# Entry of a mixture of experts: ranks by pairs, turns in three operations, squares in pieces, tokens scaled from copies

## The reference, cut to what matters

```python
x = x + g1 * mixed                                   # mixed: attention out @ w_out
hx2 = modulate(rmsnorm(x, norm_ffn_g[l]), sh2, sc2)
x = x + g2 * hierarchical_moe(hx2, ...)
# in hierarchical_moe, t = tokens x 1024
g_logits = t @ w_rg + b_rg;  g_sel = argmax(g_logits)
e_logits = (t @ w_re + b_re)[group g_sel]
top_p, top_i = top_k(softmax(e_logits), 2);  top_p /= sum(top_p)
hid = silu(t @ wg) * (t @ wu);  y = sum over experts of (hid * combine) @ wd
```

## Time and profile before

| | us |
|---|---|
| time, median of 3 runs | 772.77 |
| lowest, highest | 772.65, 773.9 |
| profiled execution, its own time | 772.82 |
| its span, first to last instruction | 770.9 |

### The profile page before, as it was taken

How to read it: one execution, slowest core, us unless ns; L and a number is a source line. 1 busy time by engine, 2 the same in 40 slices (tenths; PEclk the granted TensorE clock), 3 DMA queues, 4 the chain that set the end, 5 groups by cost and what they waited for, 6 DMA issues and landing times.

```text
span 770.9 us, 11473 instructions
## 1 busy us (share of the span) xinstructions
PE 736.4 (96%) x4534; PEld 519.1 (67%) x4538; DVE 405.3 (53%) x736; ACT 310.3 (40%) x555; POOL 29.3 (4%) x42
## 2 busy tenths in 40 slices
PE   5999999999997999999999999999999999999996
PEld 3597786454695435443454346878889999999885
DVE  2583704558746112211221137967768888888443
ACT  3463202456725011101010126566556566666333
POOL 0000020033000000000000000030000000000000
PEclk9999999999999999999999999999999999999999
DMA  9883022789689799999999998304405455495101
GB/s 375 376 335 118 13 97 110 287 317 385 267 345 371 261 428 424 431 403 425 431 429 419 420 427 324 111 1 189 168 1 179 164 205 202 142 417 218 56 0 56
DMA packets 19675, 198.97 MB, mean 258 GB/s; under 512 B 2192, under 2 KB 2704, under 8 KB 4016
## 3 DMA queue, kind: packets, MB, share of 16 engines
q1 hardware_dynamic: 18720, 194.80, 63.0%
q0 software_dynamic: 624, 3.28, 1.1%
q10 hardware_dynamic: 288, 0.30, 0.1%
HBM read 197.32 MB, written 1.05 MB: 257 GB/s over the span
## 4 chain that ended last, share of the span: by engine, by line
PE 78%; DMA 9%; DVE 5%; ACT 5%; issue 1%; POOL 1%; SPq 0%; DVEq 0%; ACTq 0%; POOLq 0%
PE banks L1610 12%; PE banks L1921 8%; PE banks L1181 7%; PE banks L1646 6%; DMA ring<-in_w_up 5%; PE banks L1883 5%; PE banks L1881 5%; PE banks L1877 5%; PE banks L1384 2%; PE banks L1139 2%; PE banks L1568 2%; DMA ring<-in_w_mod 2%; PE banks L1421 2%; PE banks L1422 2%; PE banks L1423 2%; DVE w_lo L1970 2%
## 5 line engine op out<-in xcount | busy, mean ns | idle before, releaser
L1970 DVE TENSOR_TENSOR w_lo<-ring,w_hi 128x1024 fp32r<-128x1024 f32 (+1 forms) x122 | 145.7, 1203 | 70.1 <-ACT w_hi L1055 25.3
L1610 PE MATMUL banks<-ring,att 128*64 128x512 f32 x448 | 113.9, 593 | 5.2 <-DMA ring<-in_w_up 2.9
L1610 PEld LDWEIGHTS banks<-ring,att 128*64 128x64 f32 x448 | 40.1, 137 | 61.7 <-issue 54.7
L756 ACT ACTIVATE w_hi<-ring 128x1024 fp32r<-128x1024 f32 x50 | 52.2, 1055 | 40.4 <-PE banks L1181 24.8
L2347 DVE TENSOR_TENSOR front<-front,banks 128x512 f32<-128x512 f32 x8 | 5.5, 688 | 98.8 <-PE banks L1610 98.8
L1050 ACT ACTIVATE w_hi<-ring 128x1024 fp32r<-128x1024 f32 x44 | 46.0, 1053 | 16.0 <-PE banks L1883 8.1
L1877 PE MATMUL banks<-h_hi,w_hi 128*128 128x256 f32 x320 | 44.9, 283 | 0.0
L1881 PE MATMUL banks<-h_hi,w_lo 128*128 128x256 f32 x320 | 44.9, 283 | 0.0
L1883 PE MATMUL banks<-h_lo,w_hi 128*128 128x256 f32 x320 | 44.9, 283 | 0.0
L1881 PEld LDWEIGHTS banks<-h_hi,w_lo 128*128 128x128 f32 x320 | 41.3, 192 | 0.0
L1883 PEld LDWEIGHTS banks<-h_lo,w_hi 128*128 128x128 f32 x320 | 41.3, 192 | 0.0
(11 more groups left out here) (383 smaller groups left out, 1485.2 us busy)
## 6 DMA issues: line engine op xcount, KB each, us to landing
ring<-in_w_up SPq DMA_DIRECT2D x21, 2048.0 KB, 9.6
ring<-in_w_mod SPq DMA_DIRECT2D x11, 2048.0 KB, 8.8
ring<-in_w_down SPq DMA_DIRECT2D x9, 2048.0 KB, 12.9
ring<-in_w_in SPq DMA_DIRECT2D x8, 2048.0 KB, 17.7
ring<-in_w_gate SPq DMA_DIRECT2D x8, 2048.0 KB, 14.7
ring<-in_w_up SPq DMA_DIRECT2D x12, 1024.0 KB, 7.9
ring<-in_w_down SPq DMA_DIRECT2D x9, 1024.0 KB, 14.2
big<-in_w_down SPq DMA_DIRECT2D x8, 1024.0 KB, 14.0
```

What stands on the lines that cost most here:

```text
L756: nc.scalar.activation(chunk_part(w_hi, chunk, c), chunk_src(chunk, c), ACT.Copy).then_inc(chunk_hi[stage], 1)
L1610: last = nc.tensor.matmul(bank[2 + j][CAP * e:CAP * (e + 1), :], xs[:, k, at:at + CAP], gate_or_up(n + e, k, odd), start=(k == 0), stop=(k ...
L1970: return V.tensor_tensor(dst, src, high.bitcast(F32), ALU.subtract)
```

## The change

- Products: `turn_x(4)` to `turn_x(6)` move ahead. 4 and 5 stand behind product 6, and 6 stands in the middle of product 7. `turn_x(7)` stands behind the router as before, and now also waits for squares and copies of what came earlier in its banks.
- Squares are taken in three pieces per token tile: features 0 to 511, 512 to 895, 896 to 1023 (`TOK_PIECES`). Beside them VectorE copies the unscaled tokens into `h2tok` (`tokens_copied`, six copies, `tok_a`), the two engines taking turns on a bank. Two of the three operations for the mean square are made before the last piece.
- ScalarE's four scalings out of PSUM go; the high parts are scaled while they are copied, directly behind the reciprocal, and the load of the table for Exp comes behind them. The low parts scale too (`scalar_tensor_tensor`).
- Ranks: instead of two passes of `top`, four operations on all 4 x 4 pairs of a row (160 elements for each partition) and a comparison with a constant. The maxima for the softmax come after `chosen`.
- Counts: the total stands first, in bank 2 with a signal of its own. The number of turns takes three operations. The clears of banks 4 to 7 stand before `stay_awake`, now 11; behind the counts stand three products of zeros.
- The six operations for the sums of the weights move behind the first `inputs`, into the loop (`token_weights`).
- Low parts are made and gathered with the second half of the features first. The first expert pair begins with feature tiles 4 to 7 and waits for `xs` tile pair by tile pair (`turned`).
- The constants get three tables and lose one, 48 columns more. In later turns the order of two loads and the first `inputs` follow suit.

```diff
--- before.py
+++ after.py
+        TOK_PIECES = ((0, slice(0, 512)), (1, slice(0, 384)), (1, slice(384, 512)))
...
             def rest_of_window(done):
-                expert_loads(1, done, (1, 3, 4, 5, 6, 7))
+                for n, j in ((2, 3), (4, 1)):
+                    sp.wait_ge(used, done + n)
+                    expert_load(1, j)
+                expert_loads(1, done, (4, 5, 6, 7))
...
-            for half in range(2):
-                act.wait_ge(tok_t, half + 1)
+            for n, (half, at) in enumerate(TOK_PIECES):
+                act.wait_ge(tok_t, n + 1)
                 for q in range(NT):
+                    if q == 1:
+                        act.wait_ge(tok_a, 2 * n + 1)
+                    to = (0, 2, 6)[n] + q
+                    nc.scalar.activation(att[:, 2 * half + q, at], xtok(q, half)[:, at], ACT.Square,
+                                         accum_out=rs[:, to:to + 1]).then_inc(tok_sq, 1)
...
+            act.wait_ge(tok_a, 6)
+            act.wait_ge(tok_inv, 1)
+            for half in (1, 0):
+                for q in range(NT):
+                    at = slice(half * 512, (half + 1) * 512)
+                    nc.scalar.activation(h2tok_hi[:, q, at], h2tok[:, q, at], ACT.Identity,
+                                         scale=rs[:, 4 + q:5 + q]).then_inc(tok_hi, 1)
             prefetch(ACT.Exp)
-            act.wait_ge(tok_inv, 1)
-                    nc.scalar.activation(h2tok[:, q, half * 512:(half + 1) * 512], xtok(q, half)[:, :], ACT.Identity,
-                                         scale=rs[:, 4 + q:5 + q]).then_inc(tok_a, 1)
...
-                    act.wait_ge(tok_a, 2 * q + half + 1)
-                    nc.scalar.activation(h2tok_hi[:, q, at], h2tok[:, q, at], ACT.Copy).then_inc(tok_hi, 1)
...
-                inputs(w * 16 + 1, 0, 0)
-                inputs(w * 16 + 3, 2, 4)
+                inputs(w * 16 + 1, 2, 4)
+                inputs(w * 16 + 3, 0, 0)
...
-                if k % 4 == 3:
+                if k in (3, 6, 7):
                     last.then_inc(tok_t, 1)
...
-                last = out_part(0, CHUNK1, OUT1, m, range((6, 6, 7)[m] if m < 3 else 0, KD))
+                if m < KD - 1:
+                    last = out_part(0, CHUNK1, OUT1, m, range((6, 6, 7)[m] if m < 3 else 0, KD))
+                else:
+                    out_part(0, CHUNK1, OUT1, m, range(4))
+                    turn_x(6)
+                    last = out_part(0, CHUNK1, OUT1, m, range(4, KD))
                 last.then_inc(proj_out, 1)
...
-                if m >= 2:
+                if 2 <= m < 6:
                     turn_x(m - 2)
                 if m == 5:
                     for k in range(4):
                         router(k, slice(0, T), wr_x, xT[:, k, :])
-            turn_x(6)
+                if m == 6:
+                    turn_x(4)
+                    turn_x(5)
             for k in range(4, 7):
                 router(k, slice(0, T), wr_x, xT[:, k, :])
             pe.wait_ge(resid, KD)
             router(7, slice(0, T), wr_x, xT[:, 7, :]).then_inc(logits_part, 1)
+            pe.wait_ge(tok_sq, 4)
+            pe.wait_ge(tok_a, 4)
             turn_x(7)
...
-            stay_awake(16, 2)
+            pe.wait_ge(tok_sq, 6)
+            pe.wait_ge(tok_a, 6)
+            for b in range(4):
+                clear(4 + b).then_inc(scattered_bank if b < 2 else scattered, 1)
+            stay_awake(11, 2)
             pe.wait_ge(comb_done, 1)
             first_q, second_q = (ones_and_zeros(small[:, 14, NE * q:NE * (q + 1)]) for q in range(NT))
             upper_b, ones_b = ones_and_zeros(upper), ones_and_zeros(ones)
+            nc.tensor.matmul(bank[2][:, 0:16], ones_b, first_q, start=True, stop=False)
+            nc.tensor.matmul(bank[2][:, 0:16], ones_b, second_q, start=False, stop=True).then_inc(counted, 1)
             nc.tensor.matmul(bank[3][:, 384:400], upper_b, first_q, start=True, stop=True)
             nc.tensor.matmul(bank[3][:, 400:416], ones_b, first_q, start=True, stop=False)
-            nc.tensor.matmul(bank[3][:, 400:416], upper_b, second_q, start=False, stop=True)
-            nc.tensor.matmul(bank[3][:, 416:432], ones_b, first_q, start=True, stop=False)
-            nc.tensor.matmul(bank[3][:, 416:432], ones_b, second_q, start=False, stop=True).then_inc(counted, 1)
-            for b in range(4):
-                pe.wait_ge(tok_a, (1, 2, 3, 4)[b])
-                clear(4 + b).then_inc(scattered_bank if b < 2 else scattered, 1)
-            stay_awake(3, 2)
+            nc.tensor.matmul(bank[3][:, 400:416], upper_b, second_q, start=False, stop=True).then_inc(counted, 1)
+            stay_awake(3, 1)
...
-                    if not odd:
+                    if not odd and not first:
...
+                        turned = first and j == 0 and not odd
+                        for k in (4, 5, 6, 7, 0, 1, 2, 3) if turned else range(KD):
+                            if turned and k % 2 == 0:
+                                pe.wait_ge(xs_a if k % 4 < 2 else xs_d, w * 16 + (2 if k >= 4 else 4))
                             for e in range(2):
...
-                                                        start=(k == 0), stop=(k == KD - 1))
+                                                        start=(k == (4 if turned else 0)),
+                                                        stop=(k == (3 if turned else KD - 1)))
...
                 pe.wait_ge(y_lo, w * 16 + 2)
                 pe.wait_ge(tok_hi, 4)
                 gather(0, 0, range(KD), (h2tok_hi,))
+                pe.wait_ge(tok_lo, 2)
+                gather(0, 2, range(4, KD), (h2tok_lo,))
                 pe.wait_ge(tok_lo, 4)
-                gather(0, 0, range(KD), (h2tok_lo,))
+                gather(0, 0, range(4), (h2tok_lo,))
...
+            def tokens_copied(n, qs=(1, 0)):
+                for q in qs:
+                    if q == 1:
+                        dve.wait_ge(tok_t, n + 1)
+                    else:
+                        dve.wait_ge(tok_sq, 2 * n + 1)
+                    V.tensor_copy(h2tok[:, q, 512 * half + at.start:512 * half + at.stop], xtok(q, half)[:, at]
+                                  ).then_inc(tok_a, 1)
...
+                if m in (5, 6):
+                    tokens_copied(m - 5)
+                if m == 6:
+                    dve.wait_ge(tok_sq, 4)
+                    link(V.tensor_tensor(rs[:, 4:6], rs[:, 0:2], rs[:, 2:4], ALU.add))
+                    link(V.tensor_scalar(rs[:, 4:6], rs[:, 4:6], 1.0 / D, EPS, ALU.mult, ALU.add))
...
-            dve.wait_ge(tok_sq, 4)
-            link(V.tensor_tensor(rs[:, 4:6], rs[:, 0:2], rs[:, 2:4], ALU.add))
-            V.tensor_scalar(rs[:, 4:6], rs[:, 4:6], 1.0 / D, EPS, ALU.mult, ALU.add).then_inc(var, 1)
+            tokens_copied(2, (1,))
+            dve.wait_ge(tok_sq, 6)
+            V.scalar_tensor_tensor(rs[:, 4:6], rs[:, 6:8], 1.0 / D, rs[:, 4:6], ALU.mult, ALU.add).then_inc(var, 1)
+            tokens_copied(2, (0,))
...
-            def top(of, n, onehot):
-
-                link(V.tensor_reduce(per_row(best, n), rows(of), AX, ALU.max))
-                link(V.tensor_tensor(rows(marks), rows(of), over_row(per_row(best, n)), ALU.is_equal))
-                link(V.tensor_tensor(rows(marks), rows(marks),
-                                     desc.unsqueeze(1).unsqueeze(1).broadcast_to([P, NT, 5, 4]), ALU.mult))
-                link(V.tensor_reduce(per_row(best, n + 5), rows(marks), AX, ALU.max))
-                link(V.tensor_tensor(rows(onehot), rows(marks), over_row(per_row(best, n + 5)), ALU.is_equal))
-
-            top(values, 0, ones1)
-            link(V.scalar_tensor_tensor(both_, ones1, -BIG, values, ALU.mult, ALU.add))
-            top(both_, 10, ones2)
-            link(V.tensor_tensor(both_, ones1, ones2, ALU.add))
+            link(V.tensor_tensor(pairs(worse), bc(each, 2, [P, 10, 4, 4]), bc(each, 3, [P, 10, 4, 4]), ALU.is_ge))
+            link(V.tensor_tensor(pairs(worse), pairs(worse), bc(below, 1, [P, 10, 4, 4]), ALU.mult))
+            link(V.tensor_tensor(pairs(signs), pairs(worse), worse.rearrange("p (x i j) -> p x j i", i=4, j=4), ALU.subtract))
+            link(V.tensor_reduce(rank.rearrange("p (x i) -> p x i", i=4), pairs(signs), AX, ALU.add))
+            link(V.tensor_tensor(per_token(taken), per_token(rank), bc(places, 1, [P, NT, 5, 4]), ALU.is_lt))
...
+            link(V.tensor_reduce(best, per_token(values), AX, ALU.max))
+            V.tensor_tensor(rows(added), per_token(values), bc(best, 3, [P, NT, 5, 4]), ALU.subtract).then_inc(ediff, 1)
...
-            link(V.tensor_reduce(top_n, bank[3][:, 416:432], AX, ALU.max))
-            link(V.tensor_scalar(windows_f, top_n, float(CAP), 1.0, ALU.is_gt, ALU.add))
-            for c in range(2, T // CAP):
-                link(V.scalar_tensor_tensor(windows_f, top_n, float(c * CAP), windows_f, ALU.is_gt, ALU.add))
-            link(V.tensor_scalar(turns_f[:, 2:3], windows_f, -1.0, None, ALU.add))
```

(32 more changed lines are left out.)

63 lines of the change are left out of this document (31 added, 32 removed).

## The result

The kernel took 773.31 us before and 767.17 after (medians of six runs each, taken together); the ratio is 0.9926 [0.9912, 0.9940]. Two later sets gave 0.9939 [0.9920, 0.9957] and 0.9937 [0.9923, 0.9952]. All runs of the study taken together, the kernel before averages 772.64 (83 runs, standard error 0.13) and the kernel after 767.70 (18 runs, 0.19). That is a gain of 4.9 us with a standard error of 0.2. The kernel before alone scatters from 770.7 to 776.4, so six runs alone place a gain only to about 1 us.

The account below looks back on a forecast made before the run. The experts run at the pace of DMA and TensorE, both starting from the first expert product. Terms -0.1 - 0.5 - 0.66 - 2.35 = -3.6 us take 772.82 to 769.2 us; 8-in-10 range 767.8 to 770.9.

Parts of the forecast that it names:

- The entry: Stretch up to the first expert product, from residuals through ranks, counts and gather; forecast to shorten by 3.6 us.
- Part 1: Projection and squares, to the reciprocal: last residual +0.55 us, shorter squares -0.65, together -0.1.
- Part 2: Ranks to first count: pair operations save 1.13 us, but TensorE's zeros hold the count, so -0.5 arrives.
- rival 2: TensorE's zeros are not in the way and the count follows `chosen`: another -0.65 us, 768.5; inside the forecast's 0.76.
- Part 3: Count through turns to gather: three operations fewer, turns 0.8 us after the count, gather 1.3 later; -0.66 us.
- Part 4: Gather to first expert product: 4.1 us instead of 6.44, as VectorE's `inputs` no longer hold it up; -2.35 us.
- Whatever moves that point moves the end: An earlier first expert product (250.71) passes whole to the kernel's end while DMA's empty stretch lasts, up to 5.6 us.
- ranks free, zeros not in the way: Case given for the range's lower end, 767.8 us: ranks at no cost for width, count not held by zeros.
- Rival 1: Clock falls to 1.2 GHz between projection and gather, gather and first products slow: 777 us; 0.04 with other causes of loss.
- Rival 3: VectorE's copies delay the last residual by 1 us (770.2) or pair operations cost more (770.0); both 771, 0.09 shared.
- rival 4: Gain stays in the entry because loads that do not follow the start set the experts' end: 772.5 us; 0.06.
- rival 5: Gather stays bound by the register load and the table load returns, half the gather-to-experts gain lost: 770.5 us; 0.09 shared.

Follow-up runs that it names:

- zeros7: Kernel after with 7 products of zeros ahead of the counts in place of 11; ratios 0.993 and 0.9929 to the kernel before, mean 767.38 us.
- weights_back: Kernel after with the six operations for the sums of the weights back ahead of VectorE's loop, turned order kept; one time of 767.27 us.
- zeros27: Kernel after with 27 products of zeros ahead of the counts in place of 11; ratio 0.9985 to the kernel before, mean 771.51 us.
- zeros0: Kernel after without any product of zeros ahead of or behind the counts, the four clears of banks kept; one time of 772.27 us.
- wide: Kernel before with only the table of constants 48 columns wider, as it is after the change; ratio 1.0003 to the kernel before.
- before_again: Kernel before measured and traced once more, nothing changed; ratio 0.9996 against itself.
- onepiece: Kernel after with squares in two pieces of 512 and the turns of features at their old places, copies still on VectorE; one time of 770.46 us.

## Why the prediction was right and wrong

**The entry: right in its sum, and each part within 0.15.** 3.59 was measured where 3.6 was forecast. The first expert product came at 246.63 for 247.1, because the fifth residual had come 0.49 earlier.

*Part 1.* From the fifth residual to the last one it took 10.65 for 10.04, +0.61 where +0.55 stood in the sum, and the shorter squares brought 0.78 (1.59 for 2.37 from the copy of the logits to the reciprocal) where 0.65 did.

*Part 2.* The pairs took 1.79 (237.78 to 239.57) for 1.67. One of the four, which reads the pairs in exchanged order, costs 0.44 where its sibling costs 0.32; the slope from 40 to 512 elements had given 0.36 for each. The step that mattered was the next one, and it holds: TensorE's zeros and not the ranks set the count. It came 0.88 after `chosen` began (240.45 and 239.57), 0.25 would have been enough (so in before), and zeros7 gives the 0.65 back that the prediction had named for rival 2. Rival 2 (zeros not in the way) is thereby out, and zeros7 is how it would have looked.

*Part 3.* Count to turns 0.70 for 1.29, and from the turns to the gather 1.48 for 1.49. That distance stays between 1.48 and 1.59 in every kernel here. The reading that TensorE's own register load and loop entry stand there, and not the selection matrix, fits but is not shown: the selection starts 0.30 behind the turns in each of the eighteen traces and ends 0.49 to 0.60 ahead of the gather, so no run moves one without the other. What speaks for the register is that `chosen` passed to the count in 0.06, far less than 0.49.

*Part 4.* The size was right (2.44 for 2.35), the reason was not. The step "That was late as VectorE finished the sums of the weights at 247.32 and then took 1.15 to enter its loop" explains 1.15 of the wait in the old order, yet counting on the moved sums for the gain was wrong: with the turned order they bring nothing (weights_back, 23.00 for 22.91 to 23.01). It is the order that takes VectorE's `xs` off the path.

**The end: the step that failed** is "Whatever moves that point moves the end". It holds for the start of the experts (zeros27), but the sum stopped there and put all that follows at no change. Behind it lay 0.92 us that go with a load of VectorE's code. The trace of before has that load at 769.4 to 770.0, behind the output's last bytes, and no term of the sum is made for it. With it the sum is 4.5, beside 4.9 +- 0.2 of all runs; the 0.4 that is left is within two standard errors. The clock at the start may hold it. Half of the recorded runs of the kernel before (38 of 77) have a mean granted clock of 0.997 or less, and only 2 of 18 of the kernel after. Where the mean clock was 0.998 or more, the kernels average 771.76 and 767.54, 4.2 apart. Mean clocks also contain the kernels' last microseconds, so this sorting is rough, and whether the change itself makes the early fall rarer stays open; it acts 200 us later, and three of the five traces with before's code have no fall either.

The 2.03 us between the forecast of 769.2 and the measured 767.17 are then these: 0.92 for the load of code, 0.4 that stay open, 0.18 because the sum started from one execution of 772.82 where the mean is 772.64, and 0.53 because the median of the six runs after lies below the mean of all eighteen. The last two are scatter. The range was too narrow for the same reason: its lower end of 767.8 is put down to "ranks free, zeros not in the way", which by the prediction's own terms is 768.0, and it holds no term for the scatter of a median of six. Even so the mean of all runs, 767.70, lies just below it.

Of the first comparison's 6.1 the other 1.2 is scatter. Traces of alike kernels differ in two places: up to the fifth residual (223.7 to 226.1, zeros0 left out), where the clock's fall near 19 us takes the larger part, and from the start of the experts to VectorE's last operation (514.0 to 515.5). What makes the second is not shown. Its mean is 514.75 over the five traces with before's code and 514.38 over the thirteen with after's, a difference of 0.37 with a standard error of 0.25. The waits for loads fell from 2.9 to 2.4 where a rise above 4 would have spoken against the forecast; but they are anywhere from 2.3 (wide) to 3.0 (before_again) in kernels with before's experts and from 2.4 to 3.0 (zeros27) in those with after's, so they are no sign of either.

**The rivals.** Rival 1 (clock) did not come, but it stood nearer than 0.04 suggests: with before's turns and squares it did (onepiece), and without the zeros too. Its price was too high. I had multiplied the whole gather and the time to the first released load by two, +8; zeros0 lost 2.1 between gather and experts, since the clock was at 1.00 again from 251.3, ahead of the first expert product at 252.57. Rival 3 (VectorE in the way) came to 0.06 us on the last residual and 0.12 on the ranks, the second covered by the zeros; rival 4 (gain stays in the entry) is excluded by zeros27, and rival 5's table load shows nowhere on the path.

## What to carry to other kernels

Follow the critical thread through to the last byte and past it: a load of code behind the output may cost 0.9 us and go away with six instructions more or less. Where two edits both take an operation off the path, undo each alone and both together; here one of them had the whole of the gain and the other none. Before a measured gain above the forecast is explained, the scatter of the kernel against itself has to be known: here a gain of 6.1 in one set was 4.9 in all of them. The mean granted clock of each execution, beside its time, shows where to look for that scatter.

## What the runs showed of the hardware

The length of an idle stretch of TensorE does not by itself say whether its clock falls. Idle parts of 1.20, 0.96 and 2.29 us in the kernel before left it at 1.00, with seven products of zeros and then the gather between them; 1.80 us in onepiece, and 1.61 and 1.91 with short work between them in zeros0, brought it to 0.50. By the stretches the lowered clock lasted from about 240 to 243.5 in onepiece, and from 244.5 to 251 in zeros0.

At one and the same place the length did tell. Ahead of the second group of sixteen products near 18 us, TensorE idled 0.96 to 1.91 us in ten traces, and the group took 1.92 or 1.93 us; in the other eight it idled 2.06 to 2.52 us, the clock went to 0.50, and the group took 2.51 to 3.41. The group started at 18.0 to 18.3 in all eighteen, when its load had landed. So it was not a late load that made the idle time longer, but a TensorE that had been done earlier with the group in front, which began at 13.6 to 14.1 in the eight and at 14.3 to 15.3 in the ten.

An operation of VectorE on 160 elements for each partition took 0.32 us, and 0.44 when one of its operands was read in exchanged order (238.50 in the timeline of after).
